# A hybrid decoder trunk: output projection and first norm moved into the mixers' stage, one tile behind

## The reference, cut to what matters

```
o_a = dsa_attention(q_a, k_a, v_a, q_i, k_i, w_i, topk)
o_b = hgrn2_chunkwise(q_b, logf, k_b, i_b)
o_b = rms_norm(o_b, onorm_gain) * silu(g_b)
mix = concatenate([o_a, o_b], axis=-1) @ w_out          # (1040, 1024) @ (1024, 1024)
h = layer_norm(ALPHA * h + mix, ln_mix_g[0], ln_mix_b[0])
h = layer_norm(ALPHA * h + swiglu(h, w_gate[0], w_up[0], w_down[0]), ln_ffn_g[0], ln_ffn_b[0])
```

## Time and profile before

| | us |
|---|---|
| median of three runs | 2850.94 |
| the profiled execution | 2848.14 |
| its span | 2846.4 |
| busy: TensorE / VectorE / POOL / ScalarE | 2673.8 / 1297.6 / 1054.5 / 839.6 |
| mixers, row m = 1 / 2 / 3 / 5 / 7 / 8 | 43.6 / 45.5 / 36.3 / 49.3 / 59.0 / 73.3 |
| out-projection, from the mixers' end to the trunk's first load | 153.9 |
| from there to the trunk's first product | 12.6 |

### The profile page before, as it was taken

The page is one execution under the profiler, slowest core; times in us unless marked ns, Lnnn a source line. Parts: engine busy times, 40 slices in busy tenths (PEclk is TensorE's granted clock), DMA queues, the critical chain, the costliest instruction groups (busy, mean ns, idle before and its releaser), DMA issues.

```text
span 2846.4 us, 35950 instructions
## 1 busy us (share of the span) xinstructions
PE 2673.8 (94%) x14135; PEld 2195.5 (77%) x14135; DVE 1297.6 (46%) x2469; ACT 839.6 (29%) x1367; POOL 1054.5 (37%) x628
## 2 busy tenths in 40 slices
PE   6779999689999989599999999999999999999996
PEld 5758999678777634489999877888877888888885
DVE  4889999756665423233333332332232232233224
ACT  2573222124333211222222232232232332233222
POOL 1221111356444201353333343344443344345433
PEclk9899999769999999799999998999999999999998
DMA  2001121101010030323332232233332233333331
GB/s 95 31 1 45 55 93 58 56 16 30 16 30 9 1 134 0 96 82 89 89 90 86 78 89 59 89 86 107 89 89 59 89 89 104 102 91 96 104 109 54
DMA packets 239314, 198.30 MB, mean 70 GB/s; under 512 B 9392, under 2 KB 219376, under 8 KB 239152
## 3 DMA queue, kind: packets, MB, share of 16 engines
q1 hardware_dynamic: 230960, 187.52, 22.1%
q10 hardware_dynamic: 8192, 8.52, 0.9%
HBM read 183.31 MB, written 12.71 MB: 69 GB/s over the span
## 4 chain that ended last, share of the span: by engine, by line
PE 56%; DMA 1%; POOL 1%; DVE 1%; ACT 0%; issue 0%; POOLq 0%; SPq 0%; DVEq 0%
PE banks L1678 34%; PE banks L1694 19%; PE banks L1711 1%; PE banks L1716 1%; PE banks L1728 1%; DMA raw<-in_w_up 1%; POOL wL L1603 0%; PE banks L1338 0%; ACT wH L1768 0%; DVE y L1317 0%; DVE y L1864 0%; PE banks L1713 0%; DMA draw<-in_w_down 0%; POOL y L1323 0%; DVE n_bn L1282 0%
## 5 line engine op out<-in xcount | busy, mean ns | idle before, releaser
L1678 PE MATMUL banks<-hL,wH 128*128 128x512 f32 (+1 forms) x1760 | 619.7, 352 | 25.1 <-POOL wL L1603 14.7
L1678 PE MATMUL banks<-hH,wL 128*128 128x512 f32 (+1 forms) x1760 | 619.1, 352 | 0.0
L1603 POOL TENSOR_TENSOR wL<-raw,wH 128x2048 fp32r<-128x2048 f32 x88 | 406.5, 4620 | 568.2 <-ACT wH L1768 568.2
L1678 PE MATMUL banks<-hH,wH 128*128 128x512 f32 (+1 forms) x1760 | 617.0, 351 | 0.0
L1844 DVE TENSOR_TENSOR hid<-hid,banks 128x512 f32<-128x512 f32 (+1 forms) x110 | 64.3, 585 | 781.4 <-PE banks L1678 670.5
L1678 PEld LDWEIGHTS banks<-hL,wH 128*128 128x128 f32 x1760 | 332.5, 189 | 73.8 <-issue 15.1
L1678 PEld LDWEIGHTS banks<-hH,wL 128*128 128x128 f32 x1760 | 332.5, 189 | 46.4
L1678 PEld LDWEIGHTS banks<-hH,wH 128*128 128x128 f32 x1760 | 333.0, 189 | 45.0
L1610 POOL TENSOR_TENSOR dL<-draw,dH 128x1024 fp32r<-128x1024 f32 x88 | 219.8, 2498 | 370.7 <-ACT dH L1774 370.6
L1864 DVE TENSOR_TENSOR y<-y,banks 128x512 f32<-128x512 f32 (+1 forms) x340 | 233.1, 686 | 220.7 <-PE banks L1694 219.7
L1694 PE MATMUL banks<-dH,hidL 128*128 128x512 f32 (+1 forms) x748 | 304.2, 407 | 2.3 <-issue 2.3
(11 more groups left out here) (220 smaller groups left out, 4377.5 us busy)
## 6 DMA issues: line engine op xcount, KB each, us to landing
raw<-in_w_gate SPq DMA_DIRECT2D x88, 512.0 KB, 4.6
raw<-in_w_up SPq DMA_DIRECT2D x88, 512.0 KB, 5.9
draw<-in_w_down SPq DMA_DIRECT2D x88, 512.0 KB, 3.4
slab<-in_w_in SPq DMA_DIRECT2D x10, 1024.0 KB, 5.8
va<-in_x SPq DMA_DIRECT2D x8, 512.0 KB, 4.9
vg_scratch<-relu ACTq DMA_DIRECT2D x32, 128.0 KB, 1.7
w_out_sb<-in_w_out SPq DMA_DIRECT2D x4, 1024.0 KB, 8.2
y<-in_x SPq DMA_DIRECT2D x8, 512.0 KB, 6.3
```

The source lines that it names most:

```text
L1603: nc.gpsimd.tensor_tensor(wL[:, ff % 2, :, :, :].rearrange("p g k f -> p (g k f)"), raw[:, :, :, :].rearrange("p g k f -> p (g k f)"), wH[ ...
L1678: last = nc.tensor.matmul(banks[:, GU + (2 * q + g) % 3, 0:n], wt[:, ff % 2, g, k, :], h[:, k, a:a + n], start=(k == 0 and part == 0), sto ...
```

## The change

The stage `out_projection` is gone. Its products are made in the mixers' stage, a tile in four quarters of 256 columns: quarter 0 of tile m-1 in step (m, 7), quarters 1 to 3 of tile m-2 in steps (m, 1), (m, 3) and (m, 5). A quarter of tiles 0 to 7 is a job of the bank SHARED, placed behind the step's shared job and ahead of `turn`; its reader is VectorE's `out_added`, near the end of VectorE's step. Tile 8 is multiplied in row 9 and in six added steps of a row 10, in banks 0 to 3. The weights of tiles 0 to 7 are loaded again for each quarter, in two halves of 512 KB; tile 8's go to the space of `kaT` and `va`. `oT` keeps two tiles. z, q and g have one buffer instead of two, and SP's loads are in a new order. The sums go to `y`, which now exists from the start: the scores of tiles up to 7, ScalarE's relu buffer and `qi_raw` lie in it, and x is loaded to it when the scores of a tile have been used.

Tiles 0 to 6 are normed in the mixers' stage, with `root_by_log` (Ln, then Exp of half of it) in place of Sqrt and reciprocal, one part in each of six steps; tiles 7 and 8 in pairs 0 to 3 of the trunk, with Sqrt. All tiles are transposed and split in the trunk: tiles 0 to 4 ahead of the first product, tiles 5 to 8 in pairs 0, 1, 3 and 4.

```diff
+NORMED = NT - 2
+        y = sb(top, "y", [P, NT, D])
-                score = sb(mixer, "score", [P, SC_COLS])
+                score = (y[:, :, :].rearrange("p m d -> p (m d)")[:, NT * D - SC_LAST:NT * D],
+                         sb(mixer, "score_last", [P, NKEYS[-1]]))
...
-            with stage() as c:
-                out_projection(nc, c, sem, sb, banks, ident, x, meta, ins, oT, y, hH, hL)
...
+    oT = sb(c, "oT", [P, 2, DC, P])
+    QW = D // 4
+    wq = sb(c, "w_out_part", [P, 2, DC // 2, QW])
...
-    steps = units + [(NT, h) for h in range(STEPS)]
+    steps = units + [(NT, h) for h in range(STEPS)] + [(NT + 1, h) for h in range(6)]
...
+    def out_job(m, h):
+        jobs = {7: (m - 1, 0), 1: (m - 2, 1), 3: (m - 2, 2), 5: (m - 2, 3)}
+        return jobs[h] if h in jobs and 0 <= jobs[h][0] < NT else None
+
+    def norm_tile(m, h, lag):
+        at = m * STEPS + h - lag
+        t = (at - 5) // STEPS - 2
+        return t if at >= 0 and at % STEPS == 5 and 0 <= t < NORMED else None
+
+    shared = [("qa", 0)]
+    for step in steps:
+        if shared_job(*step):
+            shared.append(shared_job(*step))
+        if out_job(*step) and out_job(*step)[0] < NT - 1:
+            shared.append(("op", *out_job(*step)))
...
+        def load_w(job):
+            for kh in range(2):
+                if job and kh == 0:
+                    sp.wait_ge(wq_read, job)
+                if job and kh == 1:
+                    sp.wait_ge(shared_psum, nth["op", (job - 1) // 4, (job - 1) % 4])
+                q = job % 4
+                sp.dma_start(wq[:, kh, :, :], w_v[:, kh * 4:kh * 4 + 4, q * QW:(q + 1) * QW]).then_inc(wq_loaded[kh], 16)
...
+        for m, h in steps:
+            if h == 0 and m + 1 < NT:
+                load_q(m + 1)
+            if h == 5 and 1 <= m < NT:
+                if m + 1 < NT:
+                    load_v(m + 1)
+                load_g(m)
+            if h == 5 and m + 2 < NT:
+                load_z(m + 2)
+            if h == 0 and m in (4, 6, 7, 8):
+                sp.wait_ge(nmax_raw, A_HEADS * m)
+                load_y(max(m, 5))
...
+            if out_job(m, h):
+                t, q = out_job(m, h)
+                if 4 * t + q + 1 < 4 * (NT - 1):
+                    load_w(4 * t + q + 1)
...
+        def quarter(m, q, bank):
+            n = TILES[m][1]
+            for k in range(DC):
+                if m == NT - 1:
+                    w = wq_last[q][:, k, :]
+                    if k == 0:
+                        pe.wait_ge(wl_loaded[q], 16)
+                else:
+                    w = wq[:, k // 4, k % 4, :]
+                    if k % 4 == 0:
+                        pe.wait_ge(wq_loaded[k // 4], 16 * (4 * m + q + 1))
+                last = nc.tensor.matmul(banks[0:n, bank, 0:QW], oT[:, m % 2, k, 0:n], w, start=(k == 0), stop=(k == DC - 1))
+                if k == DC // 2 - 1:
+                    last.then_inc(wq_read, 1)
+            return last
...
             if shared_job(m, h):
                 on_shared(*shared_job(m, h))
+            if out_job(m, h):
+                t, q = out_job(m, h)
+                if t < NT - 1:
+                    on_shared("op", t, q)
+                else:
+                    pe.wait_ge(shared_done, nth["ot_att", t])
+                    quarter(t, q, q).then_inc(op_psum, 1)
             if 1 <= i <= NU:
                 turn(i - 1)
...
+            if norm_tile(m, h, 1) is not None:
+                n0.root_by_log(act, norm_tile(m, h, 1))
+            if norm_tile(m, h, 3) is not None:
+                n0.scale(act, norm_tile(m, h, 3))
...
+        def out_added(m, q):
+            n = TILES[m][1]
+            dve.wait_ge(y_loaded[m], 16)
+            if m < NT - 1:
+                bank, done, signal = SHARED, (shared_psum, nth["op", m, q]), shared_done
+            else:
+                bank, done, signal = q, (op_psum, q + 1), op_added
+            at = y[0:n, m, q * QW:(q + 1) * QW]
+            dve.wait_ge(*done)
+            nc.vector.scalar_tensor_tensor(out=at, in0=at, scalar=ALPHA, in1=banks[0:n, bank, 0:QW], op0=ALU.mult, op1=ALU.add)\
+              .then_inc(signal, 1)
+            if q == 3 and m < NORMED:
+                dve.wait_ge(shared_done, nth["op", m, 3])
...
                 nc.vector.tensor_scalar(late, late, TAKEN_BELOW, MASKED, ALU.is_ge, ALU.mult).then_inc(late_mask, 1)
+            if out_job(m, h):
+                out_added(*out_job(m, h))
+            if norm_tile(m, h, 0) is not None:
+                n0.stats(dve, norm_tile(m, h, 0))
+            if norm_tile(m, h, 2) is not None:
+                n0.shifts(dve, norm_tile(m, h, 2))
+            if norm_tile(m, h, 4) is not None:
+                n0.gains(dve, norm_tile(m, h, 4))
...
+    def root_by_log(self, act, j):
...
+        act.wait_ge(self.var, j - self.before + 1)
+        self.nc.scalar.activation(self.std[0:n, m:m + 1], self.mv[0:n, m, 1:2], ACT.Ln).then_inc(self.rooted, 1)
+        act.wait_ge(self.rooted, j - self.before + 1)
+        self.nc.scalar.activation(self.rstd[0:n, m:m + 1], self.std[0:n, m:m + 1], ACT.Exp, scale=-0.5).then_inc(self.inverted, 1)
...
+    def first_norm(ph, i, lag):
+        return NORMED + i - lag if ph.nth == 0 and NORMED <= NORMED + i - lag < NT else None
+    def turned_at(ph, i):
+        return {0: 5, 1: 6, 3: 7, 4: 8}.get(i) if ph.nth == 0 else None
...
+                if s == 0 and ph.nth == 0:
+                    pe.wait_ge(n0.lo, 2 * (3, FIRST)[ch])
...
+        for j in range(FIRST):
+            n0.turn(pe, j)
...
             gate_up(2 * g + 1)
+            if turned_at(ph, i):
+                n0.turn(pe, turned_at(ph, i))
...
+        for j in range(3):
+            n0.high(act, j)
         high_w(0)
+        for j in range(3, FIRST):
+            n0.high(act, j)
         high_w(1)
```

More of the change, by code:

```diff
@@ L723, in _ @@
         sp.dma_start(w_qa[:, :, :], ins["w_uq"][0].rearrange("(k p) f -> p k f", p=P)).then_inc(w_loaded, 16)
[L724 to L735, removed]
+        w_v = ins["w_out"][0].rearrange("(k p) f -> p k f", p=P)
@@ new lines, in _ @@
+        sp.wait_ge(pads, 2)
+        load_z(0)
+        load_q(0)
+        sp.dma_start(gain[:, :], ins["onorm_gain"][0:1, :].to_broadcast([P, A_WIDTH])).then_inc(gain_loaded, 16)
+        sp.wait_ge(pads, 4)
+        load_v(0)
+        load_g(0)
+        load_z(1)
+        load_v(1)
+        load_w(0)
+        n0.load(sp, ins["ln_mix_g"][0], ins["ln_mix_b"][0])
+        for m in range(5):
+            load_y(m)
+        for m, h in steps:
[10 more added lines that the diff above has]
+                load_y(max(m, 5))
+            if (m, h) == (NT, 0):
+                sp.wait_ge(qk_done, NU)
+                sp.wait_ge(qk_tail, A_HEADS)
+            if (m, h) == (NT, 2):
+                sp.wait_ge(pv_done, NU)
+            if m == NT and h in (0, 2):
+                for q in (h, h + 1):
+                    sp.dma_start(wq_last[q], w_v[:, :, q * QW:(q + 1) * QW]).then_inc(wl_loaded[q], 16)
+            if out_job(m, h):
+                t, q = out_job(m, h)
+                if 4 * t + q + 1 < 4 * (NT - 1):
+                    load_w(4 * t + q + 1)
@@ L882, in on_shared @@
                                                ident[0:n, 0:n])
+            if what == "op":
+                last = quarter(m, *q, SHARED)
             last.then_inc(shared_psum, 1)
+        def quarter(m, q, bank):
[13 more added lines that the diff above has]
+            return last
         def scores_of(m, h, a, kn, at):
@@ L1514, in trunk @@
     n3 = NormSteps(nc, c, sem, sb, banks, ident, "n3", y, list(range(1, NT)), like=n1)
+    n0 = NormSteps(nc, c, sem, sb, banks, ident, "n0b", y, list(range(NT)), (PB, PB + 1), (hH, hL), like=n1,
+                   loads=(NORMED,), before=NORMED)
+    FIRST = 5
     wg = [ins["w_gate"][i].rearrange("(k p) f -> p k f", p=P) for i in range(DEPTH)]
@@ L1580, in _ @@
                 load_d(2 * g + 2)
+            if ph.nth == 0 and i == 6:
+                sp.wait_ge(n0.biased, NT - NORMED)
+                n1.load(sp, ins["ln_ffn_g"][0], ins["ln_ffn_b"][0])
             if ph.nth == 1 and i == 4:
@@ L1643, in _ @@
                 bands()
+            if first_norm(ph, i, 2) is not None:
+                n0.bias(pool, first_norm(ph, i, 2))
             for T, normed, pooled in steps_in(ph, i):
@@ L1817, in _ @@
                     n1.root(act, T)
+            if first_norm(ph, i, 1) is not None:
+                n0.scale(act, first_norm(ph, i, 1))
+            if first_norm(ph, i, 0) is not None:
+                n0.root(act, first_norm(ph, i, 0))
             if ph.nth == 3:
@@ L1887, in mix @@
             n2.stats(dve, j)
+        for j in range(FIRST):
+            n0.low(dve, j)
         for g in range(NPAIR):
@@ L1913, in _ @@
                     n1.stats(dve, T)
+            if first_norm(ph, i, 2) is not None:
+                n0.gains(dve, first_norm(ph, i, 2))
+            if first_norm(ph, i, 1) is not None:
```

(3 more changed lines are left out.)

249 lines of the change are left out of this document (111 added, 138 removed).

## The result

The changed kernel has a median of 2863.94 us (2860.80 to 2871.38), the kernel before, timed beside it, 2850.91 (2843.74 to 2853.12). The ratio is 1.0059, its 95% interval 1.0044 to 1.0074: slower by 13.0 us by the medians and by 16.3 by the means. The prediction said 2863, a change of about +13, on the slower side. The profiled execution has a span of 2862.7 against 2846.4, 16.3 us more, and a clock of 0.955 against 0.951.

What follows compares the result with a forecast made beforehand. TensorE was taken as the bound in the mixers; rows 3 to 8 112.4, rows 1 and 2 20 and tail 28.5 put the trunk's load at +7.8, the trunk adds +5.7: +13.5 us, said as 2863, range 2840 to 2885.

Steps and rivals of the forecast that it cites:

- A quarter at 3.5 us: Mixers' stage: 16 instructions of 256 columns take 3.5 us at full clock, bounds 3.4 and 3.7.
- The waits at 28.4 us in rows 3 to 8: Steps 1, 3 and 5: the quarter waits for ScalarE's copy out of bank SHARED, 18 cases, 28.4 us.
- The covered work: Adds, stats, shifts, gains, root, scale and bias costed at nothing beside a full TensorE; uncovered, 1 us a row.
- rival D: Clock falls in the new gaps: 18 waits each bring 5 us at the lower clock, +45, 2908; chance 4%.
- the one on rows 3 to 7: Sign of being right: in rows 3 to 7 every row is 17 to 20 us longer.
- Rows 1 and 2 at 20 us: Five quarters and three waits cost 13.5 us if the clock rises early, 28.9 if not; the middle, 20, taken.
- rival A: Clock rises early and stays, in rows 1 and 2 and the tail; quarters at 3.4: +2, 2853; chance 27%.
- The tail at 28.5 us: End of the mixers, last quarters and tile 8: 27.1 us after the old end plus 1.4 for clock; bounds 25 and 33.
- rival C: Streamed weights come late behind other loads in SP's one queue, each quarter waits 1 us or more: +32, 2895; chance 7%.
- the step on SP: Loads costed at nothing: weight halves issued two steps (10 us) ahead of the next quarter; two such loads took 6.0 us.
- The trunk at +5.7: Trunk: entry +0.2, turns 5 to 8 between gate_up groups 4.2, Sqrt table loads 1.3; together +5.7 us.
- Rival B: TensorE's full windows hide latency that quarters fill, mainly rows 1 to 4; half absorbed is -27, 2836; chance 15%.

Runs made afterwards that it cites:

- e1: Changed kernel with the quarter product placed behind turn and pv in the step instead of ahead of turn: 2828.61 us, ratio 0.9921 to the kernel before.
- e8: Kernel before, plus a TensorE wait ahead of turn for ScalarE's copy in steps 1, 3 and 5 of rows 2 to 8: 2922.28 us, ratio 1.0253.
- e4: Changed kernel with the last 2 MB of tile 8's weights issued behind the loads for quarter 3 of tile 7: 2861.88 us, ratio 1.004.
- e2: Changed kernel with each quarter making 2 of its 8 source matmuls, loads, waits and adds kept: 2784.17 us, ratio 0.9763 to the kernel before.
- e5: Changed kernel with the quarter product placed between turn and pv: 2844.20 us, ratio 0.9975 to the kernel before.
- e10: e1 with TensorE waiting ahead of turn for ScalarE's copy in steps 1, 3 and 5 of rows 2 to 8: 2884.83 us, ratio 1.0125.

## Why the prediction was right, and which terms were off

**A quarter at 3.5 us: right.** e1's rows 3 to 6 give 14.0 to 14.2 us for four. The estimate from the fixed cost in the Trainium skill (TensorE: Matmul & The Clock Gate, section on 56 ns against 53.3 ns) was 3.45; the trace agrees for the quarter of step 7, which took 3.45 up to its successor's start, while those of e1 took about 3.6. Both are within the bounds.

**The waits at 28.4 us in rows 3 to 8: right.** By the prediction's working a row costs 14.0 plus its three waits: 17.7, 18.4, 18.8, 19.1 in rows 3 to 6. Measured are +17.7, +18.4, +18.8, +19.0. e1 takes the waits away and only the 14 stay, so their cause is shown, not argued. The profile shows less idle time than the price, 15.5 us for the 18.0 of these four rows, but against e1 they cost 17.6. The covered work (adds, stats, shifts, gains, the norm's roots) showed no cost there.

**Rows 7 and 8: 3.4 us each too low.** The forecast counted no clock in them. Two quarters of each, behind waits of 1.59 to 2.25 us, took 5.41 us instead of 3.72: 1.7 us four times, 6.8 us, which is the 6.7 that was missing. This is rival D at a small size: rows 3 to 8 came to +119.1 instead of +112.4. Of the prediction's signs of being right the one on rows 3 to 7 failed by it (row 7 was 22.9 us longer, not 17 to 20), and its sign for D, a clock under 1.00 in rows 3 to 8, came. Its reason against, that row 8 had 4.5 us of idle at a full clock, did not carry over. e8 shows how large D is without a quarter behind the wait: 74 us for 28. The Trainium skill's section on PSUM-queue cycling (same page) says that short idle spells between groups can make the clock go to and fro; the trace of e8 agrees, with 0.97, 0.88 and 0.88 in the windows of 700 to 1000 where before had 1.00. D's +45 did not come in this kernel. But in e8 waits of the same length, with other work behind them, lost about 46 us to the clock, so the 4% was low for what waits on TensorE can do.

**Rows 1 and 2 at 20 us: too high.** They cost 11.0 us (11.8 by the table, 0.8 given back ahead of it), less even than the 13.5 of an early clock. Row 2 ran at 1.00 throughout, the first half of rival A; its second half, that the clock stays, didn't come.

**The tail at 28.5 us: too low, 34.0.** The first quarter of it took 1.7 us more at the lower clock, and the last streamed quarter waited 3.9 us for weights, as SP had 2 MB in front of them. That is rival C in one place, which the step on SP left out; e4 takes it away and gets 3.8 us back. Apart from 0.4 us once, in the same row, all other weights came in time.

**The trunk at +5.7: 5.4.** From its first load to its first product are 13.7 us against 12.6 (predicted 12.8). ScalarE's first split was released by the load, not by the tiles' turns, and the load itself took 7.1 us up to it instead of 6.0; why is open. From the first product to the end are 1671.6 against 1667.3, +4.3 (predicted 5.5).

**The sum.** +6.7 in rows 3 to 8, -9.1 in rows 1 and 2, +5.5 in the tail, -0.3 in the trunk: 2.8 us above the forecast of +13.5 for the profiled execution. The mechanism was right: products on a full engine at their own price, plus the waits. That the median came out within 1 us of 2863 is luck: three terms were off by 5 to 9 us and cancelled for the most part, and by the means the change was 16.3. Rival B is refuted by e2 and by e1's 14 us a row: nothing was absorbed.

What the prediction did not do is to ask how the waits could be avoided. It named what stands behind the waiting quarter, turn and pv (0.60 and 1.24 us long in row 3, 1.04 and 2.36 in row 8), which are free to run; these are what covers ScalarE's copy when they are ahead.

## What to carry to other kernels

When a job is added that needs a bank whose reader has only just been started, put it behind work of the waiting engine that doesn't need the bank: here the same products made the kernel 0.5% slower (0.6% by the ratio) in one order and 0.8% faster in the other. Price a wait on TensorE at more than its length: 28 us of waits cost 35 us with dense products right behind them and 56 to 74 us with short ones, and the shorter waits of e5 brought no lower clock in rows 3 to 8. A stage is worth moving for its idle entry and drain, not for its busy part, and the streamed loads have to be followed through the last row too, where another stage's loads stand in the same queue.

## What the runs showed of the hardware

- Single waits of 0.7 to 2.3 us were followed by a fall of the granted clock to its lower level of 1.2 GHz, in some places and not in others: the wait of 0.69 us at 737.93 in e8 was followed by it from about 740 to 747 (0.50 in 742 to 746), while row 3 of the changed kernel had 3.1 us of idle and a clock of 1.00.
- How much clock is lost depends on what follows the wait: with 16 dense instructions of 256 columns right behind each wait it was 0.98 in 900 to 1000 us, with turn and pv first 0.91. One profiled execution of each was read, but the mean clocks of all timed runs keep the order: 0.952 to 0.956 for the changed kernel, 0.946 to 0.948 for e10, 0.933 to 0.936 for e8.
- An instruction of 256 float32 columns takes 0.22 us back to back (3.45 for 16), half of the 0.43 of 512 columns.
- In e1 the clock fell to 0.82 in 1020 to 1040 us although no quarter waited there for a copy; what brought it down is open.
